# Strassen's scheme for a fifth pair of feature tiles, with four of the seven products moved into the gate stage, in a fp32 two-layer decoder trunk

## The reference, cut to what matters

```python
h = rms_norm(x, g_ffn_pre)                                  # x: 256 tokens x 1024
f = silu(h @ w_gate) * (h @ w_up)                           # 1024 -> 2816 features
x = x + rms_norm(f @ w_down, g_ffn_post)                    # 2816 -> 1024
```

## Time and profile before

| what | value |
|---|---|
| median of 3 runs | 561.95 us (561.33 to 562.04) |
| the profiled execution, its own time | 561.91 us |
| its span, first to last instruction | 560.1 us |
| instructions in the span | 8756 |
| mean granted TensorE clock | 0.999 of full speed |

### The profile page before, as it was taken

One profiled execution on the slowest core, in us unless ns is written; L12 is line 12 of the kernel. 1 busy time (PEld: TensorE's weight loads), 2 busy tenths in 40 slices (PEclk: granted clock), 3 DMA queues, 4 the chain that ended last, 5 costly groups with the idle time before them and its releaser, 6 DMA issues.

```text
span 560.1 us, 8756 instructions
## 1 busy us (share of the span) xinstructions
PE 552.8 (99%) x3352; PEld 456.0 (81%) x3352; DVE 430.1 (77%) x550; ACT 307.2 (55%) x426; POOL 223.0 (40%) x307
## 2 busy tenths in 40 slices
PE   8999999999999999999999999999999999999996
PEld 6878888888888888888888888888888888888884
DVE  6799996856857748999798998775847757679983
ACT  6676775554545353555547658574645453446630
POOL 1101132406366456692220055233065485296800
PEclk9999999999999999999999999999999999999999
DMA  8964533648466464447466344425665555525411
GB/s 344 378 230 143 199 106 160 232 161 311 164 222 209 168 221 152 151 169 283 181 246 218 135 170 151 185 85 220 230 258 187 190 201 183 219 85 215 164 63 75
DMA packets 18042, 107.34 MB, mean 192 GB/s; under 512 B 2256, under 2 KB 2640, under 8 KB 6480
## 3 DMA queue, kind: packets, MB, share of 16 engines
q1 hardware_dynamic: 18000, 106.78, 52.3%
HBM read 105.72 MB, written 1.05 MB: 191 GB/s over the span
## 4 chain that ended last, share of the span: by engine, by line
PE 88%; DVE 5%; POOL 3%; ACT 1%; issue 1%; DMA 1%; DVEq 0%; POOLq 0%
PE bank L1454 74%; PE bank L1469 7%; PE bank L1531 3%; DVE w_l L953 3%; PE bank L1516 2%; POOL mixed_crossed L603 2%; PE bank L1557 1%; PE bank L1584 1%; ACT work L761 1%; DMA work<-in_first_lead 1%; DVE work L1100 1%; POOL norms L593 1%; POOL norms L594 0%; DVE mixed_squares L1107 0%; DVE work L1044 0%
## 5 line engine op out<-in xcount | busy, mean ns | idle before, releaser
L953 DVE TENSOR_TENSOR w_l<-raw,w_h 128x2048 fp32r<-128x2048 f32 (+1 forms) x90 | 202.6, 2256 | 78.1 <-ACT w_h L672 77.8
L1454 PE MATMUL bank<-w_h,actT_h 128*128 128x512 f32 (+1 forms) x568 | 223.6, 394 | 0.2
L1454 PE MATMUL bank<-w_h,actT_l 128*128 128x512 f32 (+1 forms) x568 | 219.9, 387 | 0.0
L672 ACT ACTIVATE w_h<-raw 128x2048 fp32r<-128x2048 f32 (+1 forms) x90 | 168.5, 1878 | 93.7 <-PE bank L1454 80.3
L1454 PE MATMUL bank<-w_l,actT_h 128*128 128x512 f32 (+1 forms) x568 | 218.0, 386 | 0.0
L619 POOL COPY work<-work 32x256 f32<-32x256 f32 (+1 forms) x192 | 163.7, 853 | 125.2 <-DVE work L1168 97.8
L1454 PEld LDWEIGHTS bank<-w_h,actT_h 128*128 128x128 f32 x568 | 106.8, 188 | 23.1 <-issue 2.0
L1454 PEld LDWEIGHTS bank<-w_h,actT_l 128*128 128x128 f32 x568 | 106.7, 188 | 22.1
L1454 PEld LDWEIGHTS bank<-w_l,actT_h 128*128 128x128 f32 x568 | 106.9, 188 | 20.1
L593 POOL TENSOR_TENSOR norms<-norms,constants 128x1 f32<-128x1 f32 x8 | 4.8, 602 | 93.7 <-ACT bank L788 93.6
L761 ACT ACTIVATE work<-bank,neg_max 128x128 f32<-128x128 f32 (+1 forms) x64 | 25.9, 424 | 10.0 <-DVE neg_max L1070 9.9
(11 more groups left out here) (119 smaller groups left out, 631.8 us busy)
## 6 DMA issues: line engine op xcount, KB each, us to landing
raw<-in_w_blocks SPq DMA_DIRECT2D x90, 1024.0 KB, 4.8
gains<-in_b_in SPq DMA_DIRECT2D x8, 256.0 KB, 6.1
work<-in_first_rest SPq DMA_DIRECT2D x3, 512.0 KB, 6.0
raw<-in_second_block SPq DMA_DIRECT2D x2, 512.0 KB, 7.9
x<-in_x SPq DMA_DIRECT2D x2, 512.0 KB, 13.5
gain_b<-in_g_attn_post SPq DMA_DIRECT2D x2, 512.0 KB, 8.1
gains<-in_g_ffn_pre SPq DMA_DIRECT2D x2, 512.0 KB, 6.9
gain_b<-in_g_ffn_post SPq DMA_DIRECT2D x2, 512.0 KB, 5.6
```

The lines of the kernel that those rows point to most:

```text
L672: nc.scalar.activation(w["h"][:, slot(L, b), at:], raw[:, r, at:], ACT.Copy).then_inc(hi_ready, 1)
L953: nc.vector.tensor_tensor(w["l"][:, slot(L, b), at:], raw[:, raw_slot(L, b), at:], w["h"][:, slot(L, b), at:].bitcast(F32), ALU.subtract). ...
L1454: ins = nc.tensor.matmul(bank[BANK_OF[name]][:, 0:n], left[s][:, k, :], right[r][:, k, c * BANK:c * BANK + n], start=first and k == 0 and ...
```

## The change

Five pairs go by the scheme in place of four; the fifth is feature tiles 8 and 9, the first two of chunk 2, which were a plain "down" block. The scheme of the first four pairs is done in two steps. In the gate stage, after each of the last four chunks, stands a block "top" (1 MB, the pair's four weight quarters): DVE forms the sums with five 512-wide additions, three results in place in `raw` and T4 in `gains`; the whole block is converted, and PE does the four products that go to the product banks. In the down stage stands a block "bot": the quarters B22 and B21 are loaded again (512 KB), T4 is taken from `gains`, and PE does the other three products. The fifth pair keeps raw and sum in the down stage. So a layer has 51 blocks, of which 50 are loaded.

Order of the down stage after: down (24 matmuls), bot, bot (9 each), down, bot, bot, raw, sum (9 + 12), the four late blocks. The list of DVE has `join_first` one conversion earlier, ahead of that of the second late block, and the split of the last chunk's features behind that of the third.

```diff
+for c in range(FFN_CHUNKS):
+    CHUNK_AT += [len(BLOCKS)]
...
+    if c >= 2:
+        TOP_AT += [len(BLOCKS)]
+        BLOCKS += [("top", 2 * (c - 2), 2, 0, D)]
-FAST = 4
-FAST_CHUNKS = 2
...
+FAST = TOPS + 1
+FAST_CHUNKS = 3
+for k in (10, 12):
+    BLOCKS += [("down", k, 2, 0, D)]
+    for _ in range(2):
+        BOT_AT += [len(BLOCKS)]
+        BLOCKS += [("bot", 2 * len(BOT_AT) - 2, 2, 0, D)]
+RAW_AT = len(BLOCKS)
+BLOCKS += [("raw", 2 * TOPS, 2, 0, D), ("sum", 2 * TOPS, 2, 0, D)]
```

SP, ACT (`hi`) and DVE (`lo`, and the new `add_top`):

```diff
+                if BLOCKS[b][0] == "bot":
+                    top = STORED.index(TOP_AT[BOT_AT.index(b)])
+                    sp.dma_start(raw[:, r, 0:2 * BANK], w_blocks[L, top, :, 2 * BANK:4 * BANK]).then_inc(raw_in[r], 16)
...
+                elif m == "top":
+                    r = raw_slot(L, b)
+                    act.wait_ge(tops_ready, TOPS * L + TOP_AT.index(b) + 1)
...
+                elif m == "bot":
+                    nc.scalar.activation(w["h"][:, slot(L, b), 0:2 * BANK], raw[:, r, 0:2 * BANK], ACT.Copy)
+                    nc.scalar.activation(w["h"][:, slot(L, b), 2 * BANK:3 * BANK], t4_kept[BOT_AT.index(b)], ACT.Copy
+                                         ).then_inc(hi_ready, 1)
...
+            def add_top(L, n):
+                dve.wait_ge(raw_in[r], raw_done(L, b))
+                nc.vector.tensor_tensor(b22, b22, b12, ALU.subtract)
+                nc.vector.tensor_tensor(b12, b11, b12, ALU.subtract)
+                link(L, nc.vector.tensor_tensor(t4, b21, b11, ALU.subtract))
+                nc.vector.tensor_tensor(t4, t4, b22, ALU.subtract)
+                nc.vector.tensor_tensor(b21, b22, b11, ALU.add).then_inc(tops_ready, 1)
```

DVE's list in the gate stage and behind it:

```diff
+                    if 2 <= c < FFN_CHUNKS - 1:
+                        add_top(L, c - 2)
                     if c == FFN_CHUNKS - 1:
-                        add_squares(L, 0)
                         swiglu(L, c, 0)
...
+                        if c == FFN_CHUNKS - 2:
+                            add_top(L, TOPS - 1)
...
+                    if c >= 2:
+                        after(L, TOP_AT[c - 2])
...
+                after(L, FIRST_DOWN)
+                after(L, BOT_AT[0])
+                add_squares(L)
+                after(L, BOT_AT[1])
+                after(L, BOT_AT[1] + 1)
+                after(L, BOT_AT[2])
                 join_first(L)
+                after(L, BOT_AT[3])
+                after(L, RAW_AT)
                 lo_f(L, FFN_CHUNKS - 1, 0)
                 lo_f(L, FFN_CHUNKS - 1, 1)
-                after(L, RAW_AT[3])
-                after(L, RAW_AT[3] + 1)
+                after(L, RAW_AT + 1)
                 join_second(L)
```

PE:

```diff
+            def top(L, n):
+                summed(L, n)
+                pe.wait_ge(lo_ready, L * NB + b + 1)
+                product(m1, a11, b11, n == 0, False)
+                product(m6, s2, t2, n == 0, False)
+                product(m5, s1, t1, n == 0, False)
+                product(m7, s3, t3, n == 0, False).then_inc(block_used, 1)
+            def bottom(L, n):
+                pe.wait_ge(lo_ready, L * NB + b + 1)
+                product(x12, s4, b22, False, False)
+                product(x11, a12, b21, False, False)
+                product(x21, a22, t4, False, False).then_inc(block_used, 1)
```

More of the change, by code:

```diff
@@ L51 @@
 FFN_CHUNKS = -(-FF // BANK)
-for c in range(FF // BANK):
-    BLOCKS += [(m, k, 4, c * BANK, BANK) for m in ("gate", "up") for k in (0, 4)]
+CHUNK_AT = []
+TOPS = 4
+TOP_AT = []
+for c in range(FFN_CHUNKS):
+    CHUNK_AT += [len(BLOCKS)]
+    if c < FF // BANK:
+        BLOCKS += [(m, k, 4, c * BANK, BANK) for m in ("gate", "up") for k in (0, 4)]
+    else:
+        BLOCKS += [("both", k, 4, c * BANK, BANK) for k in (0, 4)]
+    if c >= 2:
+        TOP_AT += [len(BLOCKS)]
+        BLOCKS += [("top", 2 * (c - 2), 2, 0, D)]
 LAST = FFN_CHUNKS - 1
 LAST_COLS = FF - LAST * BANK
-BLOCKS += [("both", k, 4, LAST * BANK, BANK) for k in (0, 4)]
 FIRST_DOWN = len(BLOCKS)
 KF = FF // P
-FAST = 4
-FAST_CHUNKS = 2
[L65 to L70, removed]
+FAST = TOPS + 1
+FAST_CHUNKS = 3
+BOT_AT = []
+for k in (10, 12):
[5 more added lines that the diff above has]
+BLOCKS += [("raw", 2 * TOPS, 2, 0, D), ("sum", 2 * TOPS, 2, 0, D)]
 FIRST_LATE = len(BLOCKS)
@@ L75 @@
 NL = len(LOADED)
+STORED = [b for b in LOADED if BLOCKS[b][0] != "bot"]
 PROJ_COLS = [(4 * GROUP, 256), (3 * GROUP, BANK), (GROUP, BANK), (0, BANK), (2 * GROUP, BANK)]
@@ L118, in completes @@
     m, k0, nk, col, n = BLOCKS[b]
-    if m in ("down", "raw", "sum"):
+    if m in ("down", "raw", "sum", "top", "bot"):
         return [("down", t, c) for c in range(2)] if k0 + nk == KF else []
@@ new lines, in squares_of, with summed @@
+            def squares_of(L, b):
+                return ({s: w[s][:, slot(L, b), q * BANK:(q + 1) * BANK] for s in "hl"} for q in range(4))
+            def summed(L, n):
+                pe.wait_ge(f_lo_ready, F_PARTS.done(L, (n // 2, 1)))
+                pe.wait_ge(s_lo_ready, FAST_CHUNKS * L + n // 2 + 1)
+            def top(L, n):
+                b = TOP_AT[n]
+                m1, m6, m5, m7 = products
+                a11, _, _, s1, s2, s3, _ = parts_of(n)
+                t1, b11, t3, t2 = squares_of(L, b)
+                summed(L, n)
[4 more added lines that the diff above has]
+                product(m7, s3, t3, n == 0, False).then_inc(block_used, 1)
+                USED.tick(b)
@@ L1484, in squares @@
-                t1, t3, t2, t4 = ({s: w[s][:, slot(L, b + 1), q * BANK:(q + 1) * BANK] for s in "hl"} for q in range(4))
-                pe.wait_ge(f_lo_ready, F_PARTS.done(L, (c, 1)))
-                pe.wait_ge(s_lo_ready, FAST_CHUNKS * L + c + 1)
+                a11, a12, a22, s1, s2, s3, s4 = parts_of(n)
+                _, b11, b22, b21 = squares_of(L, b)
+                t1, t3, t2, t4 = squares_of(L, b + 1)
+                summed(L, n)
                 pe.wait_ge(lo_ready, L * NB + b + 1)
-                product(m1, a11, b11, first, last)
```

146 lines of the change are left out of this document (78 added, 68 removed).

## The result

| | before | after |
|---|---|---|
| median of the runs beside each other | 562.06 us (561.25 to 562.23) | 563.0 us (561.86 to 564.13) |
| ratio, 95% interval | | 1.0018 [1.0012, 1.0024] |
| the profiled execution, its own time | 561.91 us | 562.32 us |
| its span | 560.1 us | 560.5 us |

One of the 22 executions of the kernel after ran at a granted clock of 0.56 and took 932 us; it is left out of the range and the ratio.

The account below looks back on a forecast made before the run. PE was taken as the bound, time going by its number of matmuls. Six fewer save 1.36 us and DVE, ACT and DMAs add nothing: 561.91 - 1.36 = 560.55, median 0.04 higher, 560.6 us; range 560.0 to 562.6.

Parts of the forecast that it names:

- The saving: PE, gate and down stage: three matmuls less per layer, 6 x 0.2267 = 1.36 us in all.
- Rival (3): Gate stage: bank changes cost PE a quarter to half a matmul each, giving 562.4 to 564.2 us; chance 0.07.
- DVE in the gate stage: Chunks 2 to 4: added sums and conversions fit PE's 24.48 us; last top's low part has 2.2 us margin.
- The lag: Gate stage: DVE ends chunk 1's conversions 7.5 us after PE began chunk 2, and this doesn't grow.
- the down stage's slot order: Down stage: sum block, late blocks and joins are all ready in time, with 1.3 to 1.9 us to spare.
- the DMAs at nothing: Down stage: four more 512 KB loads per layer, 4.8 us each to land, cost nothing, even at 7.9 us.
- R: Down stage: the moment at which PE ends block "raw", from which the prediction counts its times.
- (1): Down stage: the last exchange, POOL's 16 copies, comes late, from 18.4 us on; at 21.3, 566.5 us; chance 0.13.
- (2): Gate stage: DVE falls behind; a stall of about 0.7 us per layer eats the gain, 561.9 us; chance 0.18.
- The rule against the change: Gate stage: POOL's copies lock DVE out, 11 us per layer, 584 us; left out of the sum, counted with (2).

Follow-up runs that it names:

- the kernels with places of their own: Against the kernel after, three of four bots load into idle `gain_b` and `work`: 560.72 us; with the tops' sums also made one chunk earlier: 560.70 us.
- the first experiment: POOL's 16 exchange copies became one of 128 partitions, crossing left out, against the kernel after: 561.21 us, ratio 0.9989.
- the control from the kernel before: POOL's 16 exchange copies cut to one, crossing left out, against the kernel before the change: 562.59 us, ratio 1.001.

## Why the prediction was wrong

**The saving: right.** Six matmuls fewer at 0.2267 us: where nothing waits, the time came out at 560.7 us, the 560.6 of the sum. Rival (3), bank changes that cost PE time, falls with that: the kernels with places of their own have all its bank changes and the common pace (2.72 us for 12 matmuls of a top).

**DVE in the gate stage: right in busy time, short in lag.** Forecast was 21 to 23.5 of 24.5 us, measured 20.85 to 21.45, and no top was late. The lag was given as 7.5 us and not growing; `add_top` in chunk 4 began at 203.67, 8.1 after PE began the chunk. The last `add_top` should have ended 29.0 after that and ended at 30.4, because exchange 3, grown from 10.82 to 19.17 us, ended at 217.66, ACT's split waited for it and DVE for ACT (0.96 us). The exchanges of the gate stage stood in no sum of the prediction; only the last one did. The last top's low part came at 34.6 instead of 33.2, wanted at 35.4: 0.8 us of the 2.2 of margin were left. The low part of the first plain block, 1.5 us later than worked out, is what issues the second plain block's load.

**The step that failed: the down stage's slot order and the DMAs at nothing.** "Its slot order gives: the sum block's copy starts when the second plain block is used (R - 6.1)." With R at 254.7 us it started at R - 4.2. The step asked when the slot is free and not when DVE would have the sums. A row that could have warned was in the group read for prices: ACT waited 10.8 us for loads into `raw` in the kernel before, too, though only 3.4 of them in the down stage, 1.7 per layer, for a late block. The paragraph on DMAs priced each bot's landing by itself, and well (4.2 us for 512 KB on the page of after, 4.8 taken), and never walked the load behind the bots: freed by the first plain block's low part at 232.6, landed at 238.0, converted by 242.1. From there DVE's list gives the sums at 250.5. The lag of the gate stage has its share in this, since either alone leaves the sum block in time: without the bots' loads, but with the lag, its low part ends at R - 1.3 (253.9 us, in that kernel); with POOL's copies shortened, but with the loads, at R - 1.0 (253.8 us). Everything behind was late by the same 2 us: the sum block's low part at R + 0.2 (forecast R - 1.9), the joins done at R + 5.1 (R + 3.3), the second late block at R + 7.3 (R + 5.5; wanted R + 6.8, and 0.3 later behind the first gap). A margin of 1.3 to 1.9 us was all there was for it.

**The rivals.** (1) did not happen: the last exchange took 14.77 us, 15.3 forecast, 18.4 needed. It was near all the same: it began at R - 10.5, 3.4 us later than worked out, and ended at R + 4.3, where by the prediction's own count R + 4.5 would have decided. (2) was nearest: about 0.7 us per layer, half of it at the second late block that it named, in the profiled execution. Its cause was half of it. DVE did fall behind in the gate stage, and with POOL's copies shortened it enters 2 us earlier and most of the loss goes. But the lag becomes a stall only through the load that waits for it: without the bots' loads in the buffers' turn, the lag stays and the stall is gone. The range ended at 562.6, and the median is beyond it since the sum that gave 561.9 for (2) stopped at a tie. Where the rest of the loss arises is not shown; margins of 0.7 us and less, with landings that differ by half a microsecond between executions (5.22 and 5.74 us for the same load in two profiles), may lose in several places.

**The rule against the change.** The Trainium skill (SBUF — State Buffer, section "SBUF: two separate sides") has the port pair of DVE and GpSimd as an exclusive lock whose loser fully blocks. The trace agrees: beside one long copy of POOL, an addition of DVE ends 0.54 us after the copy does, about the 0.57 us that it takes alone (the rows stand at the end of this document). The prediction set it aside for DVE because a mean over all conversions showed nothing of it. The rows do: a 512-wide addition takes 0.57 us from start to start alone (222.11 to 222.68) and 0.80 beside a copy (222.68 to 223.48); a conversion 2.17 (198.29 to 200.46) and 2.40 (201.27 to 203.67). That is some 0.2 us for each of these DVE instructions, where the prediction took the copy's whole 0.32 us for every copy. With the wait behind exchange 3 it came to 2.0 us up to the last `add_top` of layer 0, as the first experiment measured it; the 11 us per layer that were worked out for it are far too much, and nothing was too little.

## What to carry to other kernels

When a change puts short blocks into a stream of loads, walk the whole turn of the buffers: issue, landing, both conversions, next issue; and set it against PE's time for the blocks that one turn covers, since a turn with no slack carries each delay on to whatever stands last. A DMA share of 0.19 is no sign that loads are not the bound, as they may be waiting for buffers. Idle memory elsewhere, here a gain and a work tile, can turn such a loss back into the gain it was meant to be.

## What the runs showed of the hardware

One long copy of POOL held up a single instruction of DVE, until the copy ended. In the kernel with one copy of 128 partitions, DVE's timeline,

```profile
219.96 0.65 DVE L1231 TENSOR_TENSOR raw<-raw 128x512 f32<-128x512 f32 x1
220.53 1.53 DVE L1232 TENSOR_TENSOR raw<-raw 128x512 f32<-128x512 f32 x1
```

and POOL's:

```profile
220.16 1.36 POOL L636 COPY work<-work 128x1024 f32<-128x1024 f32 x1 [20.60 <-DVE work L1196]
```

The addition that starts during the copy takes 1.53 us in place of 0.65 and ends 0.5 us after the copy does. So one long copy stalls a single instruction for 0.9 us, where 16 short ones add 0.2 us to each of many. That would also explain why the control from the kernel before is no faster: there the 1024-wide addition that meets POOL's copy takes 2.06 us, against 1.42 at its place before (216.12 us). It was not tried apart.

The other surprise, loads of half a row making the kernel 0.9 us slower than loads of the whole row, has been measured twice and not explained.
